# Moving the overlay buffers of a two-block transformer kernel by one to seven words

## The chip, the cores and the metric

One Trainium2 chip, one of its cores. The metric is the device time of one execution in microseconds (us); the time of a kernel is the median of its runs.

## The reference, cut to what matters

`reference()` runs two small models in a row, all in float32, on 512 tokens of width 1024 (and 256 context tokens in the first one).

```python
def reference(x, c, ctx, c_ctx, ...):
    x = first_block(x, c, ctx, c_ctx, ...)     # layer 0: MLA attention, layer 1: gated linear attention
    return second_block(x, ...)                # layer 0: S5 + gMLP mixers, layer 1: short conv; a conv FFN in each
...
    q = (rms_norm(cq, q_norm_g) @ w_uq).reshape(b, n, MLA_HEADS, MLA_NOPE + MLA_ROPE)
...
        h = h + mix
        h = h + conv_ffn(rmsnorm(h, ffn_norm_g[layer]), ffn_w_up[layer], ffn_conv_w[layer],
                         ffn_conv_b[layer], ffn_w_down[layer])
```

Almost all the arithmetic is in products of an activation (1024, 384, 256 or 2816 wide) with a weight matrix.

## The kernel before, in words

Activations lie transposed: 128 features on the partitions, tokens along the free dimension, so an activation of 1024 features is 8 slices of 128 x 512 (or 128 x 768 where the context belongs to it).

**Products of hi and lo parts.** A float32 product is made of three passes of a faster matmul type (fp32r): every operand `x` is split into `hi`, rounded by ScalarE, and `lo = x - hi`. `product` (L427 to L432) issues them: `hi` of the activation with `hi` of the weight (L430, by the names that the profile gives to its source line; the sides are swapped for some products), then the two mixed ones (L431, L432). Activations are split by ScalarE's `high` (L792 is the helper that records its copies) and VectorE's `low` (L1116 is the helper that records its tensor_tensor instructions) from `hf`, a small buffer that holds the unsplit slice. The pairs are `Hhi/Hlo`, `Chi/Clo`, `Ahi/Alo` (by far the most used), `ghi/glo` and `Fhi/Flo`.

**Weights.** SyncE streams units of 128 x 1024 words into `raw` (5 slots); ScalarE rounds each to `whi` (L775, 3 slots), GpSimd subtracts to `wlo` (L1100, 3 slots), TensorE reads both.

**Order.** The class `Plan` writes out by hand the list of PSUM tiles in order; each of four PSUM tiles of two banks is taken in turn. All engines follow that order through semaphores that count up. Nothing in the order depends on an address.

**Buffers.** Those that live for the whole program are allocated first, by `sb`: `raw`, `whi`, `wlo`, `X`, `vec`, `ident`, `ones`, `hf`, `sq`, `acc`, `rstd` and small ones. The rest, the overlay, are put at an offset of their own, in words of 4 bytes, behind these by `place`, and different phases of the program use the same bytes under different names. `place(at, name, shape)` opens a dummy tensor of `at` words, allocates the buffer behind it, and closes both again, so that the next call starts at the same base. For example:

```python
        Hhi, Hlo = place(8704, "Hhi", [KD, N], fp22), place(14848, "Hlo", [KD, N], fp22)
        Ahi, Alo = place(20992, "Ahi", [KD, N], fp22), place(27136, "Alo", [KD, N], fp22)
        ghi, glo = place(2048, "ghi", [KD, T], fp22), place(6144, "glo", [KD, T], fp22)
        Fhi, Flo = place(0, "Fhi", [FH, T], fp22), place(5632, "Flo", [FH, T], fp22)
```

In the gated linear attention, seven masked levels per head are computed by L617 with two operands of 128 x 128 float32 each. Both operands of a level `l` lie in `level_ex[l % 3]`: for two levels in three in a slot of the overlay buffer `ex`, for every third one in `sq`, which is one of the fixed buffers:

```python
        level_ex = [ex[:, 0, :, :], ex[:, 1, :, :],
                    sq[:, :, :].rearrange("p a t -> p (a t)")[:, 0:2 * T].rearrange("p (i t) -> p i t", i=2)]
        decayed_kT = [kT[:, :], sq[:, 0, :]]
```

In the same way L634 reads `decayed_kT[0]` from the overlay and `decayed_kT[1]` from `sq`.

## Time and profile before

| | |
|---|---|
| median of 3 runs | 2364.3 us (2363.39 to 2366.1) |
| the profiled execution, own time | 2368.89 us |
| its span, first to last instruction | 2367.1 us |
| mean granted TensorE clock in it | 0.928 of full speed |
| instructions in the trace | 27756 |

The span is 1.8 us shorter than the execution's own time, and that execution 4.6 us longer than the median of the runs. In the profile TensorE's matmuls are PE, its weight loads PEld, VectorE is DVE, ScalarE ACT, GpSimd POOL.

### The profile page before, as it was taken

How to read it: one execution, taken by the hardware profiler on the slowest of the kernel's cores; microseconds unless marked ns; L12 is line 12 of the kernel's file. 1: busy time of each engine (PE TensorE's matmuls, PEld its weight loads, DVE VectorE, ACT ScalarE, POOL GpSimd, SP SyncE). 2: the span in 40 equal slices, each digit the busy share in tenths (PEclk: the TensorE clock that was granted, in tenths of full speed). 3: DMA queues.
4: the chain of work that ended last, by engine and by line, in shares of the span. 5: the costliest groups of instructions: out<-in, count | busy, mean ns of one | idle time of the engine just before them, and what ended most of it. 6: DMA issues, size and time to landing. Idle time of an engine off the chain costs nothing.

```text
span 2367.1 us, 27756 instructions
## 1 busy us (share of the span) xinstructions
PE 2066.5 (87%) x10852; PEld 1683.4 (71%) x10852; DVE 1143.4 (48%) x1717; ACT 819.1 (35%) x1113; POOL 689.7 (29%) x304
## 2 busy tenths in 40 slices
PE   4899999999969789778484879999979997999997
PEld 3787878778858677667273658788758875878875
DVE  3331666666457577576699243313332524331332
ACT  3253232332233444543331243324332324332332
POOL 1121000000312232232135424444333542444442
PEclk9799999999979799889697989999989998999998
DMA  7111111111111101112120213332222321322321
GB/s 277 36 54 45 63 54 63 55 63 63 63 47 39 33 28 45 36 29 92 34 69 18 80 63 98 89 98 90 89 80 81 99 89 57 103 85 92 99 82 52
DMA packets 46545, 167.72 MB, mean 71 GB/s; under 512 B 5424, under 2 KB 5552, under 8 KB 46160
## 3 DMA queue, kind: packets, MB, share of 16 engines
q1 hardware_dynamic: 44496, 159.93, 21.1%
q10 hardware_dynamic: 1920, 6.02, 0.7%
q8 instruction: 87, 1.43, 0.2%
q14 instruction: 42, 0.34, 0.0%
HBM read 163.83 MB, written 2.10 MB: 70 GB/s over the span
## 4 chain that ended last, share of the span: by engine, by line
PE 72%; DVE 20%; ACT 5%; issue 2%; DMA 1%; ACTq 0%; POOL 0%; DVEq 0%
PE ps L430 19%; PE ps L431 19%; PE ps L432 19%; PE ps L527 4%; PE ps L537 3%; DVE ex L1116 2%; PE ps L558 2%; DVE hf L1116 2%; DVE acc L1116 2%; DVE sq L1116 2%; DVE Alo L1116 1%; DVE hf L1122 1%; ACT sq L792 1%; DVE tmp L1116 1%; PE ps L464 1%
## 5 line engine op out<-in xcount | busy, mean ns | idle before, releaser
L1100 POOL TENSOR_TENSOR wlo<-raw,whi 128x1024 fp32r<-128x1024 f32 x253 | 616.5, 2449 | 1550.2 <-ACT whi L775 1550.2
L430 PE MATMUL ps<-Ahi,whi 128*128 128x512 f32 (+1 forms) x1328 | 529.8, 399 | 43.9 <-issue 23.5
L431 PE MATMUL ps<-Alo,whi 128*128 128x512 f32 (+1 forms) x1328 | 522.8, 394 | 0.0
L432 PE MATMUL ps<-Ahi,wlo 128*128 128x512 f32 (+1 forms) x1328 | 517.0, 389 | 0.0
L775 ACT ACTIVATE whi<-raw 128x1024 fp32r<-128x1024 f32 x253 | 259.9, 1055 | 701.2 <-PE ps L432 680.2
L430 PEld LDWEIGHTS ps<-Ahi,whi 128*128 128x128 f32 x1328 | 257.6, 194 | 121.8 <-issue 38.9
L432 PEld LDWEIGHTS ps<-Ahi,wlo 128*128 128x128 f32 x1328 | 257.3, 194 | 54.1
L431 PEld LDWEIGHTS ps<-Alo,whi 128*128 128x128 f32 x1328 | 258.3, 194 | 47.8 <-issue 0.2
L1122 DVE SCALAR_TENSOR_TENSOR cv<-ps,vec,cv 128x511 f32<-128x511 f32 (+1 forms) x176 | 131.9, 750 | 320.6 <-ACT cv L792 315.9
L430 PE MATMUL ps<-Fhi,whi 128*128 128x512 f32 x416 | 167.3, 402 | 12.9 <-DVE Flo L1116 12.8
L431 PE MATMUL ps<-Flo,whi 128*128 128x512 f32 x416 | 165.5, 398 | 0.0
L1116 DVE TENSOR_TENSOR X<-ps,X 128x512 f32<-128x512 f32 x48 | 33.3, 693 | 270.9 <-PE ps L432 270.9
L432 PE MATMUL ps<-Fhi,wlo 128*128 128x512 f32 x416 | 164.0, 394 | 0.0
L792 ACT ACTIVATE Pr<-ps,small 128x768 f32<-128x768 f32 (+1 forms) x96 | 72.9, 760 | 197.3 <-DVE small L1245 119.2
L527 PE MATMUL ps<-K,Q 96*128 96x256 f32 (+1 forms) x320 | 119.4, 489 | 8.3 <-ACT Pr L792 4.8
L537 PE MATMUL ps<-V,PT 128*128 128x64 f32 x896 | 110.7, 269 | 0.3 <-DVE PT L1269 0.3
L537 PEld LDWEIGHTS ps<-V,PT 128*128 128x128 f32 x896 | 107.5, 192 | 0.4 <-issue 0.4
L430 PEld LDWEIGHTS ps<-Fhi,whi 128*128 128x128 f32 x416 | 79.0, 190 | 37.6 <-DVE Flo L1116 20.1
L1245 DVE TENSOR_REDUCE small<-ps 128x1 f32<-128x768 f32 (+1 forms) x96 | 74.9, 780 | 50.0 <-PE ps L527 46.2
L452 PE MATMUL ps<-acc,ones 128*128 128x512 f32 (+1 forms) x36 | 26.8, 860 | 80.5 <-DVE acc L1116 80.5
L430 PE MATMUL ps<-Hhi,whi 128*128 128x512 f32 x224 | 80.9, 361 | 14.6 <-issue 9.0
L432 PEld LDWEIGHTS ps<-Fhi,wlo 128*128 128x128 f32 x416 | 79.3, 191 | 18.2
(231 smaller groups left out, 3227.3 us busy)
## 6 DMA issues: line engine op xcount, KB each, us to landing
raw<-in_units SPq DMA_DIRECT2D x301, 512.0 KB, 3.6
X<-in_xT ACTq DMA_DIRECT2D x1, 2048.0 KB, 12.8
out_xT<-X SPq DMA_DIRECT2D x8, 256.0 KB, 2.0
CX<-in_ctxT ACTq DMA_DIRECT2D x1, 1024.0 KB, 15.1
masks<-in_masks ACTq DMA_DIRECT2D x1, 512.0 KB, 3.5
gmw<-in_gmw ACTq DMA_DIRECT2D x1, 384.0 KB, 2.8
bs<-in_bs ACTq DMA_DIRECT2D x1, 384.0 KB, 3.8
vec<-in_vec ACTq DMA_DIRECT2D x1, 312.5 KB, 4.5
```

The source lines that it names most:

```text
L430: nc.tensor.matmul(out, sh, mh, start=first, stop=False)
L431: nc.tensor.matmul(out, sh, ml, start=False, stop=False)
L432: return nc.tensor.matmul(out, sl, mh, start=False, stop=last)
L527: last = nc.tensor.matmul(ps[:, o0:o0 + c1 - c0], Q[0:96, h % 2, q * P:(q + 1) * P], K[0:96, h % 2, c0:c1], start=True, stop=True)
L537: last = nc.tensor.matmul(ps[:, 0:HV], PT[:, u % 2, i * P:(i + 1) * P], V[:, t, h * HV:(h + 1) * HV], start=i == 0, stop=i == len(keys) - 1)
L558: last = nc.tensor.transpose(ps[:, i * P:(i + 1) * P], Pr[:, u % 2, i * P:(i + 1) * P], ident[:, :])
L775: nc.scalar.activation(whi[:, s % CONV, :], raw[:, c % RAW, :], ACT.Copy).then_inc(sem("whi"), 1)
L792: do(nc.scalar.activation(out, in_, f, scale=scale, **kw), sem_name)
L1100: nc.gpsimd.tensor_tensor(wlo[:, s % CONV, :], raw[:, plan.unit_at[("split", s)] % RAW, :], whi[:, s % CONV, :].bitcast(fp32), ALU.subtrac ...
L1116: do(TTi(out, x, y, op), s)
L1122: do(STTi(out, x, sc, y, op0, op1), s)
L1245: do(nc.vector.tensor_reduce(small[:, 0, u % 8:u % 8 + 1], ps[:, 0:n], AX.X, MAX, negate=True), "mx")
```

## The change

Seven thresholds are added, and `place` adds to an offset the number of thresholds that it has reached: 0 words below 5632, 7 words from 29184 on. No other line is touched.

```diff
+APART = [5632, 8704, 14336, 18432, 20992, 25088, 29184]
...
     def place(at, name, shape, dt=fp32):
 
         scope = ExitStack()
+        at += sum(at >= x for x in APART)
         if at:
             scope.enter_context(nc.sbuf_tensor(f"before_{name}", [P, at], fp32))
         t = scope.enter_context(nc.sbuf_tensor(name, [P] + shape, dt))
```

Both programs, built, have the same instructions on every engine, with the same waits, in the same order. They differ in start addresses alone. This is the programs' own table of start addresses, in bytes of a partition; `asked` is the number of words that the added line gives, the last two columns are the remainders of the built starts by 64 bytes.

```
buffer              before    after   moved  asked (words)   by 64 before / after
vec (2500 bytes)     61632    61632      0     -                0 / 0
ident                64160    64160      0     -               32 / 32
hf                   65696    65696      0     -               32 / 32
sq                   71840    71840      0     -               32 / 32
acc                  81056    81056      0     -               32 / 32
raw, whi, wlo, X       (fixed buffers)   0     -                0 / 0
Fhi                  87808    87808      0     0                0 / 0
gq                   87808    87808      0     0                0 / 0
ghi                  96000    96000      0     0                0 / 0
Flo                 110336   110368     32     1                0 / 32
glo                 112384   112416     32     1                0 / 32
Hhi, V              122624   122656     32     2                0 / 32
Hlo, O, ex          147200   147232     32     3                0 / 32
gk                  155392   155424     32     3                0 / 32
kT                  164608   164640     32     4                0 / 32
Ahi, Chi            171776   171808     32     5                0 / 32
Clo                 187136   187168     32     5                0 / 32
Alo                 196352   196384     32     6                0 / 32
Q                   202496   202528     32     6                0 / 32
Pr, PT                (both moved)      32     7                0 / 32
K, tmp              220928   220960     32     7                0 / 32
masks               224000   224032     32     7                0 / 32
```

Every other buffer of the overlay follows the same pattern: 0 bytes below an offset of 5632 words, 32 bytes from there on.

Of the kernel before, what the change touches and what calls it, by code (L numbers as in the profile page):

```python
# [26 lines left out]
AHEAD = 7  # L27
EAGER = ("up", "ch", "dn", "od")
BANKS2 = 4

VECS = [("cond", 16), ("ada_b0", 48), ("ada_b1", 48), ("norm_g0", 16), ("norm_g1", 16),
# [257 lines left out]
def build(nc, a):  # L290
# [6 lines left out]
    def sem(name):  # L297
        if name not in sems:
            sems[name] = ctx.enter_context(nc.semaphore("s_" + name))
        return sems[name]  # L300
# [4 lines left out]
    def place(at, name, shape, dt=fp32):  # L305

        scope = ExitStack()
        if at:
            scope.enter_context(nc.sbuf_tensor(f"before_{name}", [P, at], fp32))
        t = scope.enter_context(nc.sbuf_tensor(name, [P] + shape, dt))  # L310
        scope.close()
        return t

    with ctx:
        PS = [ctx.enter_context(nc.psum_tensor(f"ps{i}", [P, 1024], fp32)) for i in range(BANKS2)]

# [12 lines left out]
        sel = sb("sel", [2])  # L329

        CX = place(0, "CX", [KD, TC])
        rope = place(2048, "rope", [T])
        gate0 = place(2560, "gate0", [KD, N])
        Hhi, Hlo = place(8704, "Hhi", [KD, N], fp22), place(14848, "Hlo", [KD, N], fp22)
        V, O = place(8704, "V", [TN, D]), place(14848, "O", [TN, D])
# [65 lines left out]
        def _(pe):  # L401
            at = [0]

            def tile(key):
                n = plan.index[key]
                assert n == at[0], (key, n, at[0])
                at[0] += 1
                if n >= BANKS2:
                    for name, value in plan.free[n - BANKS2]:
                        pe.wait_ge(sem(name), value)  # L410
                return PS[n % BANKS2]

# [21 lines left out]
            def linear(key, hi, lo, k_at, ready, cols, offset=0, ks=None, col0=0):  # L434

                ps = PS[plan.index[key] % BANKS2]
                ks = ks or list(range(plan.count[plan.index[key]]))
# [309 lines left out]
        def _(ac):  # L747
# [12 lines left out]
            def convert(n):  # L760

                while converted[0] < plan.nsplit:
                    s = converted[0]
                    if s >= CONV and plan.last[("split", s - CONV)] > n:
                        break
                    c = plan.unit_at[("split", s)]
                    if plan.load_after[c] > n:
                        break

                    if plan.first_use[s] > n + AHEAD:  # L770
                        break
                    ac.wait_ge(sem(f"ld{c % RAW}"), 16 * (c // RAW + 1))
                    if s >= CONV:
                        ac.wait_ge(sem("psum"), plan.last[("split", s - CONV)] + 1)
                    nc.scalar.activation(whi[:, s % CONV, :], raw[:, c % RAW, :], ACT.Copy).then_inc(sem("whi"), 1)  # L775
                    converted[0] += 1
                    split_at.append(n)

            def psum(key):
# [4 lines left out]
                if key[0] in EAGER:  # L784
                    convert(n)
                return PS[n % BANKS2]

# [925 lines left out]
```

## Rows read from the trace of the kernel before

**Rows 1.** The page: span, busy time, and the chain that ended last.

```profile
span 2367.1 us, 27756 instructions
PE 2066.5 (87%) x10852; PEld 1683.4 (71%) x10852; DVE 1143.4 (48%) x1717; ACT 819.1 (35%) x1113; POOL 689.7 (29%) x304
...
PE 72%; DVE 20%; ACT 5%; issue 2%; DMA 1%; ACTq 0%; POOL 0%; DVEq 0%
PE ps L430 19%; PE ps L431 19%; PE ps L432 19%; PE ps L527 4%; PE ps L537 3%; DVE ex L1116 2%; PE ps L558 2%; DVE hf L1116 2%; DVE acc L1116 2%; DVE sq L1116 2%; DVE Alo L1116 1%; DVE hf L1122 1%; ACT sq L792 1%; DVE tmp L1116 1%; PE ps L464 1%
```

**Rows 2.** Groups by line, PE: name, shapes xcount | busy us, mean ns | idle before.

```profile
L430 PE MATMUL ps<-Ahi,whi 128*128 128x512 f32 (+1 forms) x1328 | 529.8, 399 | 43.9 <-issue 23.5 <-DVE Alo L1116 12.6 <-POOL wlo L1100 5.6
L430 PE MATMUL ps<-Fhi,whi 128*128 128x512 f32 x416 | 167.3, 402 | 12.9 <-DVE Flo L1116 12.8
L430 PE MATMUL ps<-whi,Ahi 128*128 128x256 f32 x288 | 81.3, 282 | 3.3 <-POOL wlo L1100 3.1 <-ACT mV L792 0.2
L430 PE MATMUL ps<-Hhi,whi 128*128 128x512 f32 x224 | 80.9, 361 | 14.6 <-issue 9.0 <-DVE Hlo L1116 5.5
L430 PE MATMUL ps<-Chi,whi 128*128 128x512 f32 (+1 forms) x160 | 55.6, 348 | 1.2 <-ACT V L792 1.2
L430 PE MATMUL ps<-ghi,whi 128*128 128x512 f32 x64 | 26.4, 412 | 0.7 <-POOL wlo L1100 0.7
L430 PE MATMUL ps<-whi,Chi 128*128 128x512 f32 x24 | 9.5, 394 | 0.0
```

**Rows 3.** Instructions of L617: xcount: duration ns min/median/max, first and last start.

```profile
L617 PEld LDWEIGHTS ps<-ex x160: 186/192/338, 748.8 to 1049.7; 128*128 128x128 f32 x160
L617 PE MATMUL ps<-ex x160: 271/275/553, 748.8 to 1049.9; 128*128 128x128 f32 x160
L617 PEld LDWEIGHTS ps<-sq x64: 186/192/333, 755.1 to 1040.9; 128*128 128x128 f32 x64
L617 PE MATMUL ps<-sq x64: 273/275/554, 755.3 to 1041.0; 128*128 128x128 f32 x64
L617 PE MATMUL ps<-gq,gk x32: 270/275/275, 742.1 to 1009.9; 128*128 128x128 f32 x32
```

**Rows 4.** Timeline of PE, 833 to 848 us: start us, us of the merged run.

```profile
833.45 1.05 PE L617 MATMUL ps<-gq,gk 128*128 128x128 f32 x8
...
840.00 1.06 PE L617 MATMUL ps<-ex 128*128 128x128 f32 x8
...
846.55 1.05 PE L617 MATMUL ps<-sq 128*128 128x128 f32 x8
```

**Rows 5.** Instructions that read `gv`, PE (columns as rows 3).

```profile
L634 PE MATMUL ps<-gv,kT x40: 379/379/635, 790.6 to 1058.8; 128*128 128x256 f32 x40
L634 PE MATMUL ps<-gv,sq x40: 379/379/793, 795.7 to 1061.0; 128*128 128x256 f32 x40
```

**Rows 6.** Groups by line and form, ACT.

```profile
L792 ACT ACTIVATE ex<-ex 128x1024 f32<-128x1024 f32 x20 | 21.2, 1060 | 26.5 <-DVE ex L1116 25.9
L792 ACT ACTIVATE sq<-sq 128x1024 f32<-128x1024 f32 x8 | 8.5, 1057 | 0.3
L792 ACT ACTIVATE ex<-ex 128x768 f32<-128x768 f32 x8 | 6.8, 846 | 0.3
L792 ACT ACTIVATE sq<-craw 128x768 f32<-128x768 f32 x5 | 4.2, 846 | 0.4 <-DVE acc L1116 0.3
```

**Rows 7.** Instructions of L1116 on DVE, by tile (columns as rows 3).

```profile
L1116 DVE TENSOR_TENSOR ex<-ex,gq x28: 691/693/694, 747.3 to 1056.2; 128x512 f32<-128x512 f32 x28
L1116 DVE TENSOR_TENSOR sq<-sq,gq x8: 691/692/693, 750.7 to 1038.6; 128x512 f32<-128x512 f32 x8
L1116 DVE TENSOR_TENSOR acc<-acc,sq x49: 691/693/2719, 22.8 to 2354.1; 128x512 f32<-128x512 f32 x36, 128x768 f32<-128x768 f32 x13
L1116 DVE TENSOR_TENSOR Flo<-hf,Fhi x52: 691/692/2784, 1430.9 to 2293.5; 128x512 fp32r<-128x512 f32 x52
L1116 DVE TENSOR_TENSOR Alo<-hf,Ahi x56: 691/693/2032, 598.0 to 1977.3; 128x512 fp32r<-128x512 f32 x40, 128x768 fp32r<-128x768 f32 x16
```

**Rows 8.** Timeline of DVE and of POOL, 1840.2 to 1844 us.

```profile
1841.01 2.78 DVE L1116 TENSOR_TENSOR Flo<-hf,Fhi 128x512 fp32r<-128x512 f32 x1
1840.61 2.63 POOL L1100 TENSOR_TENSOR wlo<-raw,whi 128x1024 fp32r<-128x1024 f32 x1 [0.18 <-ACT whi L775]
```

**Rows 9.** Timeline of PE, 1502.0 to 1503.5 us.

```profile
1501.80 0.39 PE L431 MATMUL ps<-Flo,whi 128*128 128x512 f32 x1
1502.03 0.39 PE L432 MATMUL ps<-Fhi,wlo 128*128 128x512 f32 x1
1502.25 0.39 PE L430 MATMUL ps<-Fhi,whi 128*128 128x512 f32 x1
...
1503.17 0.39 PE L431 MATMUL ps<-Flo,whi 128*128 128x512 f32 x1
```

**Rows 10.** Windows, 1500 to 1700 us: PE, PEld, DVE, ACT, POOL busy (x), PEclk, DMA share, GB/s.

```profile
1500.00:1700.00 200.00, 194.94 (x840) 157.73 (x839) 61.58 (x85) 70.97 (x87) 83.80 (x36) 0.99 0.31 92
```

**Rows 11.** Instructions on the tile `masks`.

```profile
L1116 DVE TENSOR_TENSOR At<-ps,masks x4: 691/692/692, 744.7 to 1013.0; 128x512 f32<-128x512 f32 x4
L896 ACTq DMA_DIRECT2D masks<-in_masks x1: 443/443/443, 684.8 to 684.8; - x1
...
DMA to landing us min/median/max: 3.5/3.5/3.5
```

**Rows 12.** Instructions on the tile `spare`, POOL.

```profile
L1082 POOL TENSOR_TENSOR spare<-wS,tab x12: 1589/1602/1797, 1254.9 to 1280.2; 128x512 f32<-128x512 f32 x12
L1082 POOL TENSOR_TENSOR wS<-spare x6: 1589/1590/1595, 1261.9 to 1283.6; 128x512 f32<-128x512 f32 x6
```

## The prediction

> **What bounds the kernel now.** I read the page first. TensorE is busy 87% of the span, and of the chain of work that ended last 72% is TensorE; the three lines of the hi and lo products, L430 to L432, make 57% of it. VectorE is a distant second with 20%, and no other engine has more than 5% [rows 1]. So the time is set by the pace of matmuls, and in some stretches by VectorE's small steps. In a stretch where TensorE has all it needs, the start times show that pace: from the L431 that starts at 1501.80 us to the one at 1503.17 us there are six matmuls of 512 columns, so 1.37 / 6 = 0.228 us each [rows 9], at a granted clock of 0.99, the 2.4 GHz level [rows 10]. 512 columns at 2.4 GHz take 0.213 us, so some 15 ns of each matmul are not streaming. The reader is to keep this number: if addresses have any say in the matter, it must be in those 15 ns.
>
> **What the change does.** It removes no instruction, adds none, moves none, and changes no wait. It can act only through start addresses, and there the text of the change and the built program part ways. The added line asks for one to seven words, that is 4 to 28 bytes. The table of start addresses shows 32 bytes for every buffer of the overlay from an offset of 5632 words on, and nothing below. The reason can be read from the fixed buffers in the same table: `vec` takes 2500 bytes from 61632, which ends at 64132, and `ident` starts at 64160, the next multiple of 32. Tensors start at multiples of 32 bytes, the overlay's base was one, and one word or seven behind a multiple of 32 both go up to the next. So:
>
> - `Hhi/Hlo`, `Chi/Clo` and `Ahi/Alo` move together by 32 bytes. Relative to each other nothing changes: hi and lo have the same remainder as before.
> - Only for `Fhi/Flo` and `ghi/glo` is a pair split: hi stays and lo moves by 32 bytes.
> - Against the fixed buffers (`whi`, `wlo`, `X`, `hf`, `sq`), everything moved has a new remainder by 64 bytes: 32 where it was 0, or for partners at 32 the same where it was different.
>
> What there is to price is therefore one question: does an operand at remainder 32 by 64 cost anything else than one at 0?
>
> **TensorE, by twins.** The trace of before has the answer for float32 matmuls, since L617 does the same product of two 128 x 128 operands once from `ex` (remainder 0) and once from `sq` (remainder 32). The matmul's median is 275 ns for both, the weight load's 192 ns for both, and `gq,gk`, both at remainder 0, has 275 ns as well [rows 3]. Back to back, eight of them take 1.05 us from `gq,gk`, 1.06 us from `ex` and 1.05 us from `sq` [rows 4]. L634 takes its stationary operand once from `kT` (0) and once from `sq` (32): median 379 ns for both [rows 5]. Cost of the move for the float32 matmuls: 0.
>
> The hi and lo products are of type fp32r, and no such operand at remainder 32 stands in the trace. How many read a moved buffer: three for each of the 1328 + 288 + 224 + 160 + 24 = 2024 triples on A, H and C, and one (the lo part) for each of the 416 + 64 = 480 triples on F and g [rows 2], together 6072 + 480 = 6552. The nearest rows are those of L617. The last digit of rows 4 leaves open 0.01 us in eight, 1.25 ns each, in either direction: 6552 x 1.25 ns = 8.2 us. The minimum of the matmul from `sq` is 273 ns against 271 from `ex` [rows 3]; taken as a true cost of 2 ns this gives 13.1 us, the upper end. I take 0, since the medians are equal and since the spread within `ex` alone (270 for `gq,gk`, 271 for `ex`) is as large.
>
> **ScalarE and VectorE, by twins.** ScalarE takes 1060 ns on 1024 elements within `ex` and 1057 within `sq`, and 846 ns on 768 elements whether from 0 to 0 or from 0 to 32 [rows 6]. VectorE takes a median of 693 ns for `ex<-ex,gq` (all at 0), 692 ns for `sq<-sq,gq` (32 and 0 to 32), 693 ns for `acc<-acc,sq` (all at 32), and 692 and 693 ns for `Flo` and `Alo` as they are now (32 and 0 to 0) [rows 7]. After the change `Alo<-hf,Ahi` is like `acc<-acc,sq`, and `Flo<-hf,Fhi` like `sq<-sq,gq`. Both forms stand there at the same price. Cost: 0, and a digit of 1 ns on some 1700 VectorE instructions would be 1.7 us at most, mostly beside matmuls.
>
> **A stretched VectorE instruction.** One thing in these rows could look like a collision of hi and lo: `Flo<-hf,Fhi` has a median of 692 ns and a maximum of 2784 [rows 7]. The timeline shows one at 1841.01 us, 2.78 us long, that ends 0.55 us behind a GpSimd `wlo<-raw,whi` which ran from 1840.61 to 1843.24 us [rows 8]. It lost 2.78 - 0.69 = 2.09 us, and GpSimd's instruction had 2.23 us left when it began. So the partner is GpSimd, not the other half of the pair, and the move takes nothing away. If instead the remainders of hi and lo were the cause, what could be won is TensorE's whole wait for `Flo`, 12.8 us [rows 2]. By that rule the change wins 0 us here, by the other reading up to 12.8 us; the trace agrees with the rule (2.09 us lost, 2.23 us left).
>
> **The rest.** `masks` is the largest DMA to a moved buffer. It lands 3.5 us behind its issue at 684.8 us, and its first reader starts at 744.7 us [rows 11]: 56 us of cover; even twice as slow it is hidden. `wg` goes with it. GpSimd's only moved operands are `spare` and `tab`, in 18 instructions of about 1.6 us, of which no twin exists. The spread of the first group, 1797 - 1589 = 208 ns, on all 18 would be 3.7 us [rows 12], as an upper bound; GpSimd has 0% of the chain [rows 1]. I take 0.
>
> **The sum.** 0 on the profiled execution's own time, 2368.9 us, and so 0 on the median of the runs, 2364.3 us, which is my number for the changed kernel. What a measurement of this kernel can tell from no change is about 0.2%, 4.7 us.
>
> **Rivals.**
>
> *The fp32r matmuls pay for remainder 32* (slower). The place is L430 to L432, the price 1.25 to 2 ns on 6552 matmuls, nearly all on the chain: 2364.3 + 8.2 = 2372.5 us, up to 2377.4 us. It decides from 4.7 us / 6552 = 0.72 ns per matmul. For it: no fp32r operand at remainder 32 has been seen, and a cost as small as this would be hidden in the printed digits. Against it: the float32 twins in rows 3 to 5, whose operands are as wide in memory.
>
> *Hi and lo at the same remainder get in each other's way, and F and g are freed of it* (faster). Then some of the 15 ns gap is paid where TensorE goes from hi to lo or back, twice in each of 480 triples: 960 x 15 ns = 14.4 us, so 2349.9 us at most. Against it: the step from L432 to the next L430, which stays in `Fhi`, is 1502.25 - 1502.03 = 0.22 us, those that change buffer 0.23 us [rows 9]. The digit leaves at most 0.01 x 960 = 9.6 us, 2354.7 us. It decides from 4.9 ns per change of buffer. And four fifths of the triples (A, H and C) are not touched by it.
>
> *The words are moved literally after all.* Then operands start 4 to 28 bytes off. Priced by a column's time, 213 / 512 = 0.42 ns, once per matmul, it is 6552 x 0.42 = 2.7 us, 2367.0 us, still within what counts as no change. The rows above, at multiples of 32 only, can't show such a start. The table of addresses speaks against this rival.
>
> **How the numbers follow.** Forecast (nothing changes): 0.87. Fp32r matmuls pay over 0.72 ns: 0.07. F and g gain over 4.9 ns: 0.05. Literal words: 0.01, counted with no change. So faster 0.05, same 0.88, slower 0.07. The range is that of no change, 2364.3 less and plus 0.2%, widened a little at the upper side, where the first rival begins: 2360 to 2371 us. It leaves out the far ends of both rivals, together about 1 in 10.
>
> **What would show it.** In the changed kernel's profile: the median of the matmuls from `ex` (now 32) against 275 ns; six matmuls on `Fhi/Flo` in 1.37 us, and the same on `Ahi/Alo`; `Flo<-hf,Fhi` with a median of 692 ns and still a maximum near 2780; the same chain by engine. The prediction is wrong if the step between matmuls of 512 columns leaves 0.228 us by more than 1 ns, or if TensorE's clock in a stretch is granted otherwise for a reason that I don't see.

## The result: slower by 0.8%, and the profile after

The changed kernel takes 2382.9 us (2380.2 to 2388.6, 4 runs) against 2364.6 us of before (4 runs): the ratio is 1.008, with a 95% interval of 1.006 to 1.010. 18.3 us were lost, where no change was forecast. The profiled execution is the fastest of the four, with an own time of 2380.2 us; that of before, with 2368.9 us, took longer than each of its runs.

The page of the changed kernel (two lines were added ahead, so L430 to L432 are now L432 to L434):

```profile
span 2378.5 us, 27756 instructions
PE 2076.4 (87%) x10852; PEld 1679.5 (71%) x10852; DVE 1143.8 (48%) x1717; ACT 818.7 (34%) x1113; POOL 688.8 (29%) x304
...
PE 72%; DVE 19%; ACT 5%; issue 2%; DMA 1%; ACTq 0%; POOL 0%; DVEq 0%
```

Beside [rows 1] only TensorE has moved, by 9.9 us of busy time, of 11.4 us of span; VectorE, ScalarE and GpSimd are the same to 1 us. The twins hold too. L617, now L619, on its operands in `ex` (remainder 32 now) and in `sq`:

```profile
L619 PEld LDWEIGHTS ps<-ex x160: 186/192/338, 749.1 to 1050.2; 128*128 128x128 f32 x160
L619 PE MATMUL ps<-ex x160: 270/275/553, 749.2 to 1050.4; 128*128 128x128 f32 x160
L619 PE MATMUL ps<-sq x64: 271/275/422, 755.8 to 1042.0; 128*128 128x128 f32 x64
```

Medians of 275 and 192 ns, as in [rows 3]. `Flo<-hf,Fhi`, written to remainder 32, and its stretched instances are the same as in [rows 7]:

```profile
L1118 DVE TENSOR_TENSOR Flo<-hf,Fhi x52: 691/693/2776, 1432.9 to 2304.3; 128x512 fp32r<-128x512 f32 x52
```

What changed is the pace of the fp32r matmuls. In a stretch with nothing to wait for, here are the first row and the one 20 triples later, before:

```profile
1590.21 0.39 PE L430 MATMUL ps<-Ahi,whi 128*128 128x512 f32 x1
...
1603.95 0.39 PE L430 MATMUL ps<-Ahi,whi 128*128 128x512 f32 x1
```

and in the changed kernel:

```profile
1589.70 0.40 PE L432 MATMUL ps<-Ahi,whi 128*128 128x512 f32 x1
...
1603.70 0.40 PE L432 MATMUL ps<-Ahi,whi 128*128 128x512 f32 x1
```

A triple took 13.74 / 20 = 687 ns and takes 14.00 / 20 = 700 ns, 4.3 ns more per matmul. The duration column hardly shows it (0.39 and 0.40); only the distance between starts does. In the stretch from 1500 to 1700 us, which holds these rows, the granted clock is 0.99 in both [rows 10], so it is not the clock:

```profile
1500.00:1700.00 200.00, 196.38 (x836) 157.18 (x834) 58.67 (x82) 68.38 (x84) 83.71 (x36) 0.99 0.30 93
```

On F, where only lo has moved, three triples of the changed kernel take 1507.87 - 1505.78 = 2.09 us, 697 ns each, against 685 in [rows 9] (the last digit is worth some 5 ns in such a short piece; over all triples on F without a wait the medians are 687 and 693 ns):

```profile
1505.78 0.39 PE L432 MATMUL ps<-Fhi,whi 128*128 128x512 f32 x1
...
1507.87 0.40 PE L432 MATMUL ps<-Fhi,whi 128*128 128x512 f32 x1
```

How much of the loss is this? Both traces hold the same 10852 matmul records in the same order, so they can be compared one by one. Steps (from one start to the next) of fp32r matmuls that are under 300 ns in both traces, so hold no wait, are longer by 12.4 us on A, 2.5 us on A with sides swapped, 1.7 us on F, 1.4 us on C and H and 0.5 us on g: 18.4 us together. All other steps, with the waits in them, are 6.9 us shorter, and 11.5 us are left, the difference of the two spans. So the longer steps are enough for the whole loss, and the rest of the program gave some of it back. The clock did differ elsewhere: in the first 150 us it was 0.90 before and 1.00 in the changed kernel. That is in the changed kernel's favour, and it differs as much between executions that lose nothing (0.78 in two kernels below, "Distance 0" and its control).

### The profile page after: what moved, and what is told of

Same layout as the page of the kernel before. It is cut to its first block, busy times and chain, and to the rows that moved or that the text cites. A ratio compares the mean times of both kernels' runs of the same rounds, so it can differ in the third digit from the quotient of the medians.

```text
span 2378.5 us, 27756 instructions
## 1 busy us (share of the span) xinstructions
PE 2076.4 (87%) x10852; PEld 1679.5 (71%) x10852; DVE 1143.8 (48%) x1717; ACT 818.7 (34%) x1113; POOL 688.8 (29%) x304
## 4 chain that ended last, share of the span: by engine, by line
PE 72%; DVE 19%; ACT 5%; issue 2%; DMA 1%; ACTq 0%; POOL 0%; DVEq 0%
PE ps L432 19%; PE ps L434 19%; PE ps L433 19%; PE ps L529 4%; PE ps L539 3%; PE ps L560 2%; DVE hf L1118 2%; DVE acc L1118 2%; DVE ex L1118 2%; DVE Alo L1118 1%; ACT sq L794 1%; DVE hf L1124 1%; DVE tmp L1118 1%; PE ps L466 1%; DVE small L1247 1%
## 5 line engine op out<-in xcount | busy, mean ns | idle before, releaser
L432 PE MATMUL ps<-Ahi,whi 128*128 128x512 f32 (+1 forms) x1328 | 532.0, 401 | 43.0 <-issue 23.5
L434 PE MATMUL ps<-Ahi,wlo 128*128 128x512 f32 (+1 forms) x1328 | 523.0, 394 | 0.0
L432 PEld LDWEIGHTS ps<-Ahi,whi 128*128 128x128 f32 x1328 | 256.6, 193 | 121.8 <-issue 38.5
L434 PEld LDWEIGHTS ps<-Ahi,wlo 128*128 128x128 f32 x1328 | 256.7, 193 | 57.8
L432 PE MATMUL ps<-Fhi,whi 128*128 128x512 f32 x416 | 167.9, 404 | 13.0 <-DVE Flo L1118 13.0
L434 PE MATMUL ps<-Fhi,wlo 128*128 128x512 f32 x416 | 163.0, 392 | 0.0
L432 PEld LDWEIGHTS ps<-Fhi,whi 128*128 128x128 f32 x416 | 78.5, 189 | 38.2 <-DVE Flo L1118 20.1
L432 PE MATMUL ps<-Hhi,whi 128*128 128x512 f32 x224 | 80.8, 360 | 14.5 <-issue 9.0
L434 PEld LDWEIGHTS ps<-Fhi,wlo 128*128 128x128 f32 x416 | 79.2, 190 | 19.1
## 6 DMA issues: line engine op xcount, KB each, us to landing
CX<-in_ctxT ACTq DMA_DIRECT2D x1, 1024.0 KB, 15.2
```

The source lines that it names most:

```text
L432: nc.tensor.matmul(out, sh, mh, start=first, stop=False)
L434: return nc.tensor.matmul(out, sl, mh, start=False, stop=last)
```

## The experiments

The theory at this point (A) was the first rival of the prediction: an fp32r operand at remainder 32 costs. B says that only operands that differ by 64 cost, C that any change of layout can.

**Everything moved by 64 bytes instead of 32.**

```diff
+MOVE = 16
...
         scope = ExitStack()
+        at += MOVE if at >= 5632 else 0
```

> Every overlay buffer from 5632 words on is moved by 64 bytes instead of 32; nothing else. In the changed kernel the 512-column fp32r matmuls on Ahi/Alo step 700 ns per triple against 687 before, those on Fhi/Flo 693 against 687, which accounts for nearly all of the 18 us. Theory A (a start at remainder 32 by 64 bytes costs): as before, 2364.6 us, within 2 us, and triples of 687. Theory B (relative place of the two operands by 64): the same. Rival C (the steps of TensorE lock into one of several patterns by chance of the layout, and any move can do it): a time different from before by 5 us or more in either direction.

Measured: 2383.2 us, ratio 1.0078 (1.0062 to 1.0093). 20 triples on A take 13.94 us. A and B in their plain form fall: all remainders by 64 are those of before, and it is as slow as the changed kernel.

**The whole memory moved by 32 bytes.**

```diff
+        sb("lead", [8])
         raw = sb("raw", [RAW, UT * P])
```

> The buffers of before, all of them (fixed and overlay), moved by 32 bytes by a pad of 8 words ahead of raw. Theory A (an operand of an fp32r matmul that starts at remainder 32 by 64 costs some 4.3 ns, whichever its partner): all 7512 fp32r matmuls pay, 7512 x 4.3 = 32 us, 2397 us; more if moving and stationary operand each cost. Theory B (only operands that differ by 64 cost): 2364.6 us, as before. A value between says that one of the two operands is the one that counts.

Measured: 2365.2 us, ratio 0.9987 (0.9977 to 0.9996); 20 triples 13.73 us:

```profile
1590.03 0.39 PE L431 MATMUL ps<-Ahi,whi 128*128 128x512 f32 x1
...
1603.76 0.39 PE L431 MATMUL ps<-Ahi,whi 128*128 128x512 f32 x1
```

Every address has changed, and the pace has not. A, with 2397 us, is out by far. So C in its plain form falls as well: what counts is where buffers lie to one another.

**Only the upper part moved by 32 bytes.**

```diff
         scope = ExitStack()
+        at += 8 if at >= 20992 else 0
```

> Only overlay buffers from 20992 words on (Ahi/Alo, Chi/Clo, Q, K, tmp) moved by 32 bytes; Fhi/Flo, ghi/glo, Hhi/Hlo stay where they were before. Theories A and B: 1328 triples on A at 13 ns, 288 swapped ones at 12 ns, 160 on C at 8 ns = 17.3 + 3.5 + 1.3, at most 22 us, less what is hidden by waits: 2380 us (15 of the 18 us). If the split pairs Fhi/Flo and ghi/glo were the cause instead: 2364.6 us.

Measured: 2379.5 us, ratio 1.0054 (1.0039 to 1.0069); 20 triples on A 14.00 us. About two thirds of the loss come from A and C, with no split pair in the program.

**The matmul by itself, first grid.** A new kernel of some 80 lines: buffers filled once, then TensorE alone. Its core:

```python
def run(movs, stas, cols=512, n=N):
    bank = PS[at[0] % 8]
    at[0] += 1
    for i in range(n):
        m, s = movs[i % len(movs)], stas[i % len(stas)]
        last = nc.tensor.matmul(bank[:, 0:cols], st[s][:, s // 4 + (i % 8) * P:s // 4 + (i % 8) * P + P],
                                mv[m][:, m // 4:m // 4 + cols], start=i == 0, stop=i == n - 1)
```

`m` and `s` are byte offsets, `mv` and `st` the moving and the stationary buffers, `N` is 24.

> The disputed cost by itself: a stream of fp32r matmuls, 24 of each kind, 128x512 moving, started at 14 byte offsets (0 to 128) in buffers that lie at multiples of 256, with the stationary operand at 6 byte offsets; then triples of mixed offsets, 256-column ones, and float32 ones at 0 and 32. Nothing of the reference is computed. Theory A: a step of about 229 ns at moving offsets 0, 64 and 128 and about 233 at 32 and 96, whatever the stationary offset. Theory B: 233 ns where moving and stationary offset differ by 32, 229 where both are at 32. Rival C: no regular dependence. Of the offsets between (4 to 60) no theory says more than that they cost at least as much as 32. Float32 ones: the same step at 0 and 32.

Its fp32r steps ran from 226.7 to 237.7 ns, so the cost is there while no other engine works and no data are loaded. Neither A nor B describes them: moving and stationary both at 32 take 227.9 ns, both at 0 226.7, moving at 32 or 128 on stationary 0 233.3. But for multiples of 32 moving less stationary offset does: 64 gives 228.8 as 64 - 0, as 96 - 32 and as 128 - 64. The float32 matmuls don't show it at the four pairs of offsets that were run (0 and 32 on 0 and 32). A float32 matmul leaves two records, and the starts of these groups of 8 matmuls, 16 records, are 6.87, 6.86 and 6.87 us apart:

```profile
546.85 7.03 PE L80 MATMUL ps<-pm0b,ps0b 128*128 128x512 f32 x16
553.72 7.03 PE L80 MATMUL ps<-pm32b,ps0b 128*128 128x512 f32 x16
560.58 7.03 PE L80 MATMUL ps<-pm0b,ps32b 128*128 128x512 f32 x16
567.45 7.03 PE L80 MATMUL ps<-pm32b,ps32b 128*128 128x512 f32 x16
```

This gave theory D: the **distance**, the start of the overlay's operand less that of `whi`, sets the step. By the table of addresses and the sizes of the buffers ahead of `vec`, `whi` starts at 20672 and `wlo` at 32960, both 192 past a multiple of 256, and `Ahi` at 171776, a multiple of 256. So the distance, by 256, is 64 bytes before, 96 in the changed kernel for all that moved, 128 in the kernel moved by 64. (Where the sides are swapped, `whi` is the moving operand, and moving less stationary is the negative of this: 192 before, 160 after.)

**Second grid**, with each buffer at a multiple of 4096.

> The second grid, all buffers at multiples of 4096 bytes so that no base confounds it: moving offsets 0 to 480 in steps of 32 and twelve others, stationary offsets 0, 32, 64 and 256; then fewer columns (384, 256, 128), shorter weight loads (96, 64, 32 columns of the stationary operand), and alternating pairs. Nothing of the reference is computed. Theory D: for multiples of 32 the step depends on moving less stationary offset alone, so rows for the stationary offsets are the same row shifted; 226.7 at 0, 228.8 at 64, 233.3 at 32, 96, 128. If the two read streams of TensorE meet, the dependence shrinks with the length of the weight load and is gone at 32 columns; if the moving start alone costs, it stays. With fewer moving columns the extra 6.6 ns stays the same if it is paid once per matmul.

Groups of 24; the start of a group less that of the one before, by 24, is the step:

```profile
63.65 5.77 PE L58 MATMUL ps<-m32b,s0b 128*128 128x512 f32 x24
69.25 5.67 PE L58 MATMUL ps<-m64b,s0b 128*128 128x512 f32 x24
74.76 5.77 PE L58 MATMUL ps<-m96b,s0b 128*128 128x512 f32 x24
80.37 5.76 PE L58 MATMUL ps<-m128b,s0b 128*128 128x512 f32 x24
...
213.90 5.76 PE L58 MATMUL ps<-m0b,s32b 128*128 128x512 f32 x24
219.50 5.61 PE L58 MATMUL ps<-m32b,s32b 128*128 128x512 f32 x24
224.94 5.77 PE L58 MATMUL ps<-m64b,s32b 128*128 128x512 f32 x24
230.54 5.67 PE L58 MATMUL ps<-m96b,s32b 128*128 128x512 f32 x24
```

`m32b` on `s0b` takes 5.60 / 24 = 233.3 ns, `m32b` on `s32b` 5.44 / 24 = 226.7. Worked out in this way, from the start times in ns and without the first three steps of each group:

```
moving offset      stationary 0      32      64     256
      0                 226.7     233.3   233.4   226.7
     32                 233.3     226.7   233.4   233.4
     64                 228.8     233.4   227.2   228.8
     96                 234.0     228.8   233.4   234.0
    128                 233.3     234.0   228.8   233.4
    256                 227.2     233.4   233.3   227.2
    320                 228.8     233.4   227.2   228.8
      4                 236.8     236.7   233.3   236.8
     16                 231.7     226.7   234.7   231.7
     20                 240.0     239.9   238.7   240.0
     60                 226.7     226.7   226.7   226.7
```

For multiples of 32 the step depends on the difference alone, within 0.5 ns, and it repeats after 256 bytes. 0 is best, 64 next, everything else costs 6.6 ns or more. 160 to 224 lie at 233.3 to 234.4. Starts off a multiple of 32 follow no rule that these rows show: 4 and 20 are the worst of all, 12 and 28 on stationary 0 (not printed here) take 228.9 and 226.7 ns, and 60 is at the best value throughout.

**Distance 0 in the full kernel**, a candidate for a better one.

```diff
+        small2 = sb("small2", [2])
+        eps1 = sb("eps1", [2])
         raw = sb("raw", [RAW, UT * P])
...
-        small2 = sb("small2", [2])
-        eps1 = sb("eps1", [2])
```

> The two small buffers small2 and eps1 (32 bytes each) are allocated ahead of raw instead of behind rstd: raw, whi, wlo, X, vec and hf move by 64 bytes, the overlay stays where it was. Call distance the start of an overlay operand less that of whi, by 512 bytes: 64 before, 96 in the changed kernel, 128 in the one moved by 64 bytes, 64 in the one moved as a whole, here 0. Theory D (distance sets the step of fp32r matmuls): the grid had 226.7 ns at distance 0, 228.8 at 64, 233.3 to 234 at 96 and 128. So 2.1 ns less on 7512 matmuls: 15.8 us faster than before, less what waits give back, 2350 us. Rival E (only moving away from the layout of before costs, nothing is to be won): 2365 us or more.

Measured: 2360.6 us against 2364.2, ratio 0.9984 (0.9975 to 0.9993). Faster than before, but by some 3.5 us and not 15.8. A ratio this near 1 proves little by itself: the memory moved as a whole, at the same distance as before, had 0.9987. What speaks for a gain are the steps, and that all 11 runs (2357.3 to 2363.0 us) lie below all 10 of the control that follows (2364.0 to 2369.9 us):

```profile
1590.17 0.39 PE L430 MATMUL ps<-Ahi,whi 128*128 128x512 f32 x1
...
1603.77 0.39 PE L430 MATMUL ps<-Ahi,whi 128*128 128x512 f32 x1
```

The triples on A do take 13.60 / 20 = 680 ns. Averaged over all undisturbed steps of 512 columns, A goes from 229.0 ns (in the control below) to 227.3 and F from 229.0 to 226.9, 6.2 and 2.6 us on 3672 and 1248 matmuls. C and H, whose triples alternate between 512 and 256 columns, gain nothing (matmul by matmul they lose 1 us against the control), and the 864 swapped ones of 256 columns go from 115.0 to 119.9 ns and give 4.2 us back. All undisturbed fp32r steps together are 3.4 us shorter than in the control, whose median is 5.0 us higher; the rest isn't traced.

**Control: `mod` and `sc1`, 512 bytes, ahead of `raw`.** The edit has the form of the last one.

> Control: mod and sc1 (384 + 128 bytes) are allocated ahead of raw, so raw, whi, wlo, X and hf move by 512 bytes against the overlay. Distance by 512 stays 64. Theory D: as before, 2366 us, triples of 687 ns on Ahi/Alo. If the whole distance counts (a larger period than 512), or any change of layout: another time, 2380 us as in the other moved ones.

Measured: 2365.6 us, ratio 1.0007 (0.9998 to 1.0016), 20 triples 13.73 us. As theory D says.

**The words as the text asks for them.**

```diff
-        at += sum(at >= x for x in APART)
+        words = sum(at >= x for x in APART)
...
-        t = scope.enter_context(nc.sbuf_tensor(name, [P] + shape, dt))
+        n = int(np.prod(shape))
+        t = scope.enter_context(nc.sbuf_tensor(name, [P, n + words], dt))
         scope.close()
-        return t
+        if len(shape) == 1:
+            return t[:, words:words + n]
...
```

Against the changed kernel; the cut part gives views of more dimensions the same offset.

> What the text of the change asks for: the overlay buffers start literally one to seven words (4 to 28 bytes) further, as views with that offset in wider buffers that start where those of before did. Distances 84 and 88 for Ahi/Alo, 84 for Chi/Clo, 72 and 76 for Hhi/Hlo, 68 for Flo and glo. The grid showed offsets of 4 to 28 bytes at 227 to 237 ns without an order that I could name. Theory D bounds it: 7512 x (226.7 - 229 to 237 - 229), 2347 to 2425 us; I expect slower than before, 2380 us. If the built 32 bytes were worse than the asked words: 2366 us.

Measured: 2399.2 us, ratio 1.015 (1.0136 to 1.0164). 20 triples on A take 14.13 us, 707 ns. These seven offsets are worse than the 32 bytes that were built, so the rounding spared the change the larger loss. That is no rule for starts off a multiple of 32 (see 12, 28 and 60 in the grid), and the distances of this kernel, 68 to 88 bytes, are no rows of the grid; theory D, which is about multiples of 32, doesn't foresee its time.

**The fixed buffers moved by 32 bytes, the overlay not.**

```diff
+        sel = sb("sel", [2])
         raw = sb("raw", [RAW, UT * P])
```

`sel` is taken out further down, behind `sc1`.

> The overlay of before, untouched; the 32 bytes of sel are allocated ahead of raw instead of behind sc1, so raw, whi, wlo, X and hf move by 32 bytes. Distance (overlay operand less whi, by 256 bytes) goes from 64 to 32. Theory D with the period of 256 that the second grid shows (233.3 ns at 32, 228.8 at 64): slower by up to 4.5 ns on 7512 matmuls, 34 us, at least the 6072 on A, H and C; 2385 to 2398 us, triples on Ahi/Alo of 700 ns. Rival: only a move of the overlay costs (another partner than whi, such as PSUM or hf): 2365 us.

Measured: 2390.0 us, ratio 1.0096 (1.0077 to 1.0114); 20 triples on A 14.00 us:

```profile
1589.96 0.40 PE L430 MATMUL ps<-Ahi,whi 128*128 128x512 f32 x1
...
1603.96 0.40 PE L430 MATMUL ps<-Ahi,whi 128*128 128x512 f32 x1
```

The loss of the changed kernel and more, since here both halves of F and g pay, without one overlay address changed. The edit moves `raw`, `X` and `hf` together with `whi` and `wlo`; that it is the weights that count is taken from the grids, where nothing but TensorE's two operands is in play.

**The same 32 bytes under the changed kernel.**

> The changed kernel, its overlay untouched, with the same 32 bytes of sel ahead of raw. Distance is 64 again for Ahi/Alo, Hhi/Hlo, Chi/Clo, Flo and glo, and 32 for Fhi and ghi, which did not move. Theory D: the 18 us come back but for F and g, 480 triples at some 8 ns more: 2368 us, triples of 687 ns on Ahi/Alo and about 696 on Fhi/Flo. Rival (the overlay's own addresses cost): 2383 us, as the changed kernel.

Measured: 2368.9 us, ratio to before 1.0008 (0.9998 to 1.0017). The overlay of the changed kernel, remainders and split pairs included, costs next to nothing once `whi` and `wlo` have followed; the triples on F, with `Fhi` now at distance 32, have a median of 695 ns, as expected:

```profile
1589.62 0.39 PE L432 MATMUL ps<-Ahi,whi 128*128 128x512 f32 x1
...
1603.35 0.39 PE L432 MATMUL ps<-Ahi,whi 128*128 128x512 f32 x1
```

**Only `Alo` split from `Ahi`** (`at += 8 if at >= 25088 else 0`).

> Before, with only the buffers from 25088 words on moved by 32 bytes: Alo, K, Q, tmp and so on, but not Ahi. Hi and lo of the most used pair are now at different remainders, which is what the change's own words ask for. Distances 64 (Ahi) and 96 (Alo). The grid's stream that alternates 64 and 96 takes 232.5 ns per matmul against 229.1 for 64 alone: 10 ns per triple on 1328 triples and less on the swapped ones, 2378 us. If splitting the pair helped as such: below 2364 us.

Measured: 2378.5 us, ratio 1.0052 (1.0037 to 1.0068), 20 triples 13.87 us. Splitting the pair in itself is no help; it puts one of its halves at a bad distance.

**Third grid: which reads meet.**

> Third grid, 48 matmuls of each kind at the eight distances 0 to 224 in steps of 32: weight loads of 128, 96, 64 and 32 columns; 256 moving columns; the same weight block every time; 64 partitions; stationary operand alternating between offsets 0 and 32. Nothing of the reference is computed. If the moving stream meets the read of the next weights (theory F): the difference between best and worst distance, 7.7 ns with 128 columns of weights, falls with their number and is small at 32; it stays with the same block and with 64 partitions; alternating stationary offsets at distance 0 lose most of the good value, 226.7 goes to 230 or more. If instead only the starts of the two reads matter (rival G): the difference stays at 6 to 8 ns down to 32 columns. For 256 moving columns theory D expects distance 0 to be worse than 64 and 192, by 2 to 5 ns, which is what took back part of the gain of the kernel at distance 0 (its 864 swapped matmuls take 119.9 ns against 115.0).

```
distance                0     32     64     96    128    160    192    224
weights 128 columns  226.7  233.3  228.9  233.4  233.4  234.2  233.4  233.2
         96          230.0  233.3  233.3  231.1  231.7  230.8  228.4  228.9
         64          229.9  230.8  228.4  230.0  231.2  231.4  232.8  231.9
         32          231.7  232.9  231.8  233.3  230.7  230.3  231.0  230.1
same weight block    227.2  233.3  228.9  233.5  233.4  234.2  233.4  233.2
64 partitions        226.9  233.3  228.9  233.4  233.4  234.2  233.4  233.2
alternating 0 / 32   230.0  233.3  230.0  234.4  233.4  233.3  231.7  231.1
256 moving columns   120.0  117.7  117.8  119.8  118.6  118.7  117.8  118.3
```

The table is from the same kind of rows, 48 matmuls in a group. The first group with weights of 96 columns starts 11.05 us ahead of the next, 230 ns each:

```profile
125.51 11.21 PE L59 MATMUL ps<-m0b,s0b 128*96 128x512 f32 x48
136.55 11.36 PE L59 MATMUL ps<-m32b,s0b 128*96 128x512 f32 x48
```

The first line, at the distances of the full kernel, repeats the second grid. Between best and worst distance lie 7.5 ns with 128 columns of weights, 4.9 with 96, 4.4 with 64 and 3.2 with 32, and the order of the distances is another one each time. So the read of the weights has a part in it, as F says, but neither F (small at 32) nor G (6 to 8 ns throughout) is met. Fewer columns of weights also mean a product of fewer rows, which this run doesn't separate. Alternating stationary offsets lose half of the good value at distance 0, as F had it. But at a moving offset of 192 that stream takes 231.7 ns, less than either of its two distances alone (192: 233.4, 160: 234.2): the step isn't set by a matmul's own distance only. For 256 columns distance 0 is worse than 64 and 192 by 2.2 ns, as expected; the full kernel's swapped matmuls lost 4.9 ns, and their 115.0 ns before lie below every value of this row. That difference is open.

## Why the prediction was wrong, point by point

**What bounds the kernel, and what the change moves**: right. TensorE's pace sets the time, instructions and waits are the same, and the built starts are 32 bytes further whatever was asked. The literal words, 2399.2 us, show that this rounding mattered. The third rival priced them at 0.42 ns a matmul, 2.7 us; they cost 35 us. Its text had said that rows at multiples of 32 can't show such a start.

**ScalarE, VectorE, the stretched `Flo`, DMA, GpSimd**: right. The three other engines kept their busy times to 1 us, the maximum of `Flo<-hf,Fhi` is still 2.78 us with `Flo` at remainder 32, `masks` lands after 3.7 us against 3.5, and the group on `spare` has a median of 1597 ns against 1602.

**The step that failed** is "TensorE, by twins", in two places. First, "I take 0, since the medians are equal": the twins in [rows 3 to 5] are float32 matmuls, and the price was carried over to fp32r ones. The float32 twins are truly equal (429 ns per record at all four pairs of offsets in the first grid), and the fp32r matmul is not: 226.7 ns at distance 0 and 233.3 at 32. The text saw that no fp32r operand at remainder 32 stood in the trace, and took the nearest rows for the answer though they were of another type. A record of 429 ns for 512 columns is two cycles of the 2.4 GHz clock for each column, an fp32r step of 226.7 ns little over one; that the slower pace leaves room for what the faster one must wait for is argued from this, not shown. The reason given beside the medians was slack as well: 270 ns for `gq,gk` and 271 for `ex` are 1 ns apart, not the 2 ns that they were to excuse, and belong to two pairs of buffers.

Second, the question itself: "does an operand at remainder 32 by 64 cost anything else than one at 0?" It does not; the memory moved as a whole keeps the time. What costs is the distance between the moving operand and the weights, by 256 bytes. The table of addresses had it in view: "Against the fixed buffers (`whi`, `wlo`, `X`, `hf`, `sq`), everything moved has a new remainder". And L617's twins could not show it, because there both operands lie in the same buffer, `ex` or `sq`, at a distance of 0 by 256 in both cases. The pair `gv`, `sq` of L634 [rows 5] does have another distance than `gv`, `kT` (`gv`, at an offset of 11264 words, lies 96 by 256 from `sq` and 0 from `kT`), but it is float32, so it stayed at 379 ns.

**The size.** The first rival put 1.25 to 2 ns on 6552 matmuls and the decision at 0.72 ns. Measured: 18.3 us / 6552 = 2.8 ns on average, 4.3 ns in an undisturbed stretch on A. The bound of 2 ns from rows 3 was no bound, for the same reason. By the kernel with only the upper part moved, 12.8 us (0.54%) belong to A and C, which leaves some 5 us to F, g and H, less well known than either number. And the 15 ns of a matmul that are "not streaming" were no bound either: the best step of the grids, 226.7 ns, still leaves 13 ns above 213, and the worst, 240.0 ns, 27 ns. The starts explain 2 of the 15 ns and can add 11 more.

**The second rival**, hi and lo in each other's way, is refuted: the kernel with only `Alo` split is slower, and the repaired kernel, with F and g split, is not faster than before.

**The chances** gave 0.07 to slower, too little for a resource (TensorE's operand reads at full pace) of which no row existed. The first rival had the place (L430 to L432) and the direction right and the condition wrong, since remainder 32 in itself costs nothing. The range ended 12 us short.

## What to carry to other kernels

Where a stream of fp32r matmuls sets the time, the start of the activation and that of the weights, taken by 256 bytes, are a parameter of the kernel: moving the fixed buffers by 64 bytes gained 0.16% here (a small gain, told from noise by its control), a careless 32 bytes cost 0.8 to 1.0%, and the literal offsets of 4 to 28 bytes cost 1.5%. A change "of addresses only" is tested with controls that move everything together and that move the partner alone. And a twin in the trace is evidence only for its own type of instruction and for the pairs of buffers that it reads; compare start times over twenty instructions, since the duration column stayed at 0.39 to 0.40 us while the step went from 229 to 233 ns.

## What the runs showed of the hardware that was not expected

The step of a 512-column fp32r matmul, back to back at the 2.4 GHz level, is 226.7 to 234.4 ns by the distance of its operands where both start at multiples of 32, with a period of 256 bytes, and up to 240.0 ns where they don't. The Trainium skill, "TensorE: Matmul & The Clock Gate", section "Step-by-step: what each phase is for", says that TensorE has two independent read ports to SBUF, so that loading the next weights takes nothing from the running matmul. For float32 the runs agree as far as they go (429 ns at distances 0 and 32 to either side, the only ones run); for fp32r they don't, since the place of the weights against the moving operand changes the step by up to 7.5 ns with nothing else running. What it is that meets (memory banks, the port, a buffer of the engine) stays open: the length of the load changes the order of the distances and doesn't remove the effect.

At distance 64 the full kernel has two paces. In the profile of before, most triples on A take 687 ns, but some 260 of 1146 took 697 to 702, in the control some 20. Runs of the same program spread from 2360 to 2371 us. The traces speak against a tie between the two: the profiled execution of the control, with hardly a slow triple, took 2369.9 us, that of before 2368.9 us. What sets the pace is open. It does bear on sums like the one of 18.4 us above: against the trace of the control the undisturbed fp32r steps of the changed kernel are 26.0 us longer, and all others 15.2 us shorter.

A moving start of 60 bytes gave 226.7 ns for every stationary offset of the second grid. It was not tried in the full kernel.
